# HGRN2 levels in 32-row blocks, S5 input products in three fp32r passes, a re-cut head and moved side steps in a hybrid decoder block on one core

## The chip, the cores and the metric

The kernel runs on one core of one Trainium2 chip. The metric is the device time of one execution in microseconds (us); smaller is better. TensorE (PE) multiplies, VectorE (DVE), ScalarE (ACT) and GpSimd (POOL) work on tensors, SyncE (SP) issues most DMAs.

## What is computed

One layer of a decoder on x of 256 tokens by 2048 features, in float32:

```
h = RMSNorm(x); [q|f|i|g | u | sq|sk|sv | 3 gates] = h @ w_in     # 8 groups of 512, gates 3 x 2048
o_a = hgrn2(q, f, i, g)          # gated linear recurrence, 4 heads of 128
o_b = s5(u): bu = Bbar u per group of 16 channels (64 complex states); x_t = Abar x_{t-1} + bu_t
             y = Re(C x) + D u; GLU(gelu(y))
o_c = stick_breaking(sq, sk, sv) # w = exp(log sigmoid(z) + suffix sums of log(1 - sigmoid(z))), strictly causal
x = x + (sum_k sigmoid(gate_k) * (o_k @ w_branch[k])) @ w_out
x = x + (silu(conv(up1)) * conv(up2)) @ w_down,  up = RMSNorm(x) @ w_up
```

## The kernel before

All large products are split in two parts, fp32r high and low: for each weight block PE multiplies high by high, high by low and low by high. Weights come in pieces of 128x1024 through a ring of four buffers. For piece p SP loads `raw` (it waits until the low part of piece p-4 is made), ACT copies it into `w_hi` (it waits until PE has used piece p-4), DVE subtracts into `w_lo`, and PE waits for `lo_ready` of p+1. An output tile of 128 columns of w_in takes two pieces, 2n and 2n+1.

The stages in order: a head (tiles 0 to 3 interleaved, as x and the first pieces land), tiles 4 to 7, tiles 8 to 79 (tiles 32 to 79 are the gates), GLU, branches, w_out, w_up with the convolution, w_down. In the first 80 tiles the whole of the three mixers is done beside the projection, by an order written out by hand. Each engine has a function `mixers(n)`:

- PE calls `mixers(n)` behind tile n. The table AT says behind which tile each small product stands: the HGRN2 levels lev0 to lev8 behind tiles 12, 14, ... 28, hg_o 30, the stick-breaking scores z0 and z1 37, the suffix sums within0 and within1 41, sb_o 44, the S5 input products bu0 and bu1 43, then bu2 to bu7 at 51, 59, 67, the S5 outputs s5_y0 to s5_y3 at 50, 58, 66, 74. Each of them writes one of two PSUM pairs and is taken from it by ACT or DVE.
- ACT and DVE call `mixers(n+1)` at the end of their step n. Step n of ACT is: high parts of pieces 2n+4 and 2n+5, the reading of tile n (Copy, or Sigmoid for gates), `mixers(n+1)`. Step n of DVE is: low parts of the same two pieces, for n under 16 the reading of tile n, `mixers(n+1)`. So what stands in ACT's `mixers(42)` is ahead of the high parts of pieces 88 and 89 (tile 44), and DVE's `mixers(43)` is behind the low parts of these two.
- Each engine executes its queue in order. `link` (and `run` on ACT, `tt`, `ts`, `stt` on DVE) also waits for the instruction just issued.

The sine and cosine tables of S5 (four groups g of 128x1024) are made at the tiles of TABLE_AT: three DVE steps, and then on ACT in `mixers` of the fourth number the sine group (Sin, Abs, Sin, with a table load ahead).

What the prediction follows, by line: `level(k)` and `fp32_product` on PE (L413), the S5 input products (L539), the warm-up products (L559), the high parts (L711), `run` (L721), the reading of tiles (L739), the exponentials of the levels (L779, L780), the z copies (L813), the low parts (L1024), `tt`, `ts` and `stt` (L1048, L1051, L1055), the level factors (L1227, L1228), the reading of levels into NEAR (L1243, L1245), the subtraction of `within` (L1314).

Of the kernel before, what the change touches and what calls it, by code (L numbers as in the profile page):

```python
# [45 lines left out]
P = 128  # L46
HALF = P // 2
D_MODEL = 2048
SEQ = 256
# [53 lines left out]
TABLE_AT = [(20, 21, 22, 23), (24, 25, 26, 27), (28, 29, 30, 31), (50, 51, 58, 59)]  # L103
# [5 lines left out]
HEAD_LOADS = [("x", 0), ("w", 0, 0), ("x", 1), ("w", 1, 0), ("x", 2), ("w", 2, 0), ("x", 3), ("w", 3, 0),  # L109
              ("w", 0, 1), ("w", 1, 1), ("x", 4), ("x", 5), ("w", 2, 1), ("w", 3, 1), ("x", 6), ("x", 7)]  # L110

HEAD_SPLITS = [("x", 0), ("w", 0, 0), ("x", 1), ("x", 2), ("x", 3), ("w", 1, 0), ("x", 4), ("x", 5), ("w", 2, 0), ("x", 6), ("x", 7),
               ("w", 3, 0), ("w", 0, 1), ("w", 1, 1), ("x", 8), ("x", 9), ("x", 10), ("x", 11), ("w", 2, 1), ("w", 3, 1), ("p", 4),
               ("x", 12), ("x", 13), ("x", 14), ("x", 15)]

HEAD_STEPS = [(5, 6, 7), (8,), (9,), (10, 11)]
WARM = 13
# [15 lines left out]
def layer(nc, xT, w_in, w_glu, w_br, w_out, w_up, w_down, norm_mix, norm_ffn, hg_gain, s5_small, s5_b, s5_c,  # L133
          s5_skip, sb_gain, conv, out):
    ctx = ExitStack()
    with ctx:
# [13 lines left out]
        level_mask = sb("level_mask", [P, LEVELS, HALF], U8)  # L150
        eye_half = sb("eye_half", [P, HALF])
# [9 lines left out]
        root = sb("root", [P, SEQ])  # L161

# [63 lines left out]

        def product(name):
            return pair[M[name] % 2]
# [53 lines left out]

        block = ctx.enter_context(nc.Block())
# [5 lines left out]
        def _(sp):  # L289
# [13 lines left out]
            def w_half(p, q):  # L303
                w = slice(q * HALF_PIECE, (q + 1) * HALF_PIECE)
                sp.dma_start(raw[p][:, w], w_in[head_source(p), :, w]).then_inc(raw_landed[p] if q else S(f"w_half{p}"), 16)

            for kind, *which in HEAD_LOADS:
                (x_part if kind == "x" else w_half)(*which)
# [37 lines left out]
        def _(pe):  # L346
# [75 lines left out]
            def level(k):  # L422

                if k == 0:
                    pe.wait_ge(S("hg_k"), 1)
                    group_ready(pe, HG_Q)
                    ops = [((j * HALF, (j + 1) * HALF, (4 * b + h) * HALF, (4 * b + h + 1) * HALF),
                            T4[2][:, h, (2 * b + j) * HALF:(2 * b + j + 1) * HALF],
                            group(HG_Q)[:, h, (2 * b + j) * HALF:(2 * b + j + 1) * HALF], True, True)
                           for b in range(2) for h in range(HEADS) for j in range(2)]  # L430
                else:
                    pe.wait_ge(S("hg_factors"), 2 * k)
                    W = T4[4 + k % 2]
                    if k < LEVELS - 1:
                        ops = [((j * HALF, (j + 1) * HALF, (4 * b + h) * HALF, (4 * b + h + 1) * HALF),
# [1293 lines left out]
```

## Time and profile before

| | |
|---|---|
| median of 3 runs | 1402.94 us (1402.54 to 1403.33) |
| profiled execution, its own time | 1402.92 us |
| span of that execution, first to last instruction | 1401.4 us |
| busy share of the span | PE 99%, PE weight loads 92%, DVE 74%, ACT 54%, POOL 10% |
| chain that ended last | PE 91%, DVE 6%, ACT 2%, DMA 1% |
| read from HBM | 258.66 MB, 186 GB/s over the span |

An engine's busy time is the union of its instructions; PE's matmuls overlap one another, so a busy PE is not one at its peak. The chain is followed back from the last instruction to what released it. "<-" in a row stands between what is written and what is read, and between an idle time and what ended it.

### The profile page before, as it was taken

How to read it: one execution, taken by the hardware profiler on the slowest of the kernel's cores; microseconds unless marked ns; L12 is line 12 of the kernel's file. 1: busy time of each engine (PE TensorE's matmuls, PEld its weight loads, DVE VectorE, ACT ScalarE, POOL GpSimd, SP SyncE). 2: the span in 40 equal slices, each digit the busy share in tenths (PEclk: the TensorE clock that was granted, in tenths of full speed). 3: DMA queues.
4: the chain of work that ended last, by engine and by line, in shares of the span. 5: the costliest groups of instructions: out<-in, count | busy, mean ns of one | idle time of the engine just before them, and what ended most of it. 6: DMA issues, size and time to landing. Idle time of an engine off the chain costs nothing.

```text
span 1401.4 us, 27481 instructions
## 1 busy us (share of the span) xinstructions
PE 1394.3 (99%) x9682; PEld 1285.5 (92%) x9682; DVE 1030.6 (74%) x1409; ACT 754.0 (54%) x1050; POOL 143.4 (10%) x190
## 2 busy tenths in 40 slices
PE   9999999999999999999999999999999999999999
PEld 8999999999999999988888888888888888888888
DVE  7898866699898777776687777777777776445453
ACT  7584777654543454545555555555555554344332
POOL 1200000000000014322111111111111110000000
PEclk9999999999999999999999999999999999999999
DMA  8654545454555556665556656656656656666663
GB/s 280 191 181 168 162 153 184 147 168 165 189 178 174 195 171 223 223 192 194 170 197 196 189 186 192 192 180 193 191 187 193 190 177 194 208 185 202 194 206 109
DMA packets 75935, 261.66 MB, mean 187 GB/s; under 512 B 8736, under 2 KB 9280, under 8 KB 75872
## 3 DMA queue, kind: packets, MB, share of 16 engines
q1 hardware_dynamic: 74304, 256.41, 57.0%
q0 software_dynamic: 1424, 4.37, 1.1%
q8 instruction: 44, 0.72, 0.2%
q14 instruction: 19, 0.16, 0.0%
q10 hardware_dynamic: 144, 0.01, 0.0%
HBM read 258.66 MB, written 2.10 MB: 186 GB/s over the span
## 4 chain that ended last, share of the span: by engine, by line
PE 91%; DVE 6%; ACT 2%; DMA 1%; issue 0%; SPq 0%; ACTq 0%; DVEq 0%
PE bank L354 40%; PE bank L368 22%; PE bank L356 21%; PE bank L394 5%; DVE w_lo L1024 2%; PE pair L413 1%; PE bank L379 1%; DVE a_in L1257 0%; ACT gates L721 0%; ACT w_hi L711 0%; DMA x_first<-xT 0%; DVE tmp L1055 0%; DVE tmp L1048 0%; DVE x_first L1217 0%; ACT tmp L721 0%
## 5 line engine op out<-in xcount | busy, mean ns | idle before, releaser
L1024 DVE TENSOR_TENSOR w_lo<-raw,w_hi 128x1024 fp32r<-128x1024 f32 x496 | 584.6, 1189 | 305.3 <-ACT w_hi L711 301.5
L711 ACT ACTIVATE w_hi<-raw 128x1024 fp32r<-128x1024 f32 x496 | 508.3, 1030 | 417.0 <-PE bank L356 198.9
L354 PE MATMUL bank<-h,w_hi 128*128 128x512 f32 x1408 | 488.4, 390 | 0.0
L356 PE MATMUL bank<-h,w_lo 128*128 128x256 f32 x1408 | 397.1, 282 | 0.0
L368 PE MATMUL bank<-a_in,w_hi 128*128 128x256 f32 x2048 | 363.1, 281 | 0.5 <-DVE w_lo L1024 0.5
L368 PEld LDWEIGHTS bank<-a_in,w_hi 128*128 128x128 f32 x2048 | 311.8, 188 | 5.3 <-issue 4.6
L354 PEld LDWEIGHTS bank<-h,w_hi 128*128 128x128 f32 x1408 | 264.2, 188 | 55.4
L368 PE MATMUL bank<-a_in,w_lo 128*128 128x256 f32 x1024 | 285.5, 279 | 0.0
L356 PEld LDWEIGHTS bank<-h,w_lo 128*128 128x128 f32 x1408 | 266.1, 189 | 0.0
L354 PE MATMUL bank<-act,w_hi 128*128 128x512 f32 x660 | 228.8, 390 | 0.0
L368 PEld LDWEIGHTS bank<-a_in,w_lo 128*128 128x128 f32 x1024 | 192.5, 188 | 0.0
L356 PE MATMUL bank<-act,w_lo 128*128 128x256 f32 x660 | 186.1, 282 | 0.0
L354 PEld LDWEIGHTS bank<-act,w_hi 128*128 128x128 f32 x660 | 123.8, 188 | 26.0
L356 PEld LDWEIGHTS bank<-act,w_lo 128*128 128x128 f32 x660 | 124.7, 189 | 0.0
L1653 POOL TENSOR_TENSOR padded<-sum_u,rstd 128x256 f32<-128x256 f32 x88 | 73.7, 838 | 413.3 <-DVE sum_u L1045 400.5
L354 PE MATMUL bank<-a_in,w_hi 128*128 128x512 f32 x256 | 88.8, 390 | 0.0
L356 PE MATMUL bank<-a_in,w_lo 128*128 128x256 f32 x256 | 72.2, 282 | 0.0
L964 ACT ACTIVATE silu<-convd 128x256 f32<-128x256 f32 x43 | 17.9, 417 | 96.0 <-DVE convd L1512 96.0
L1510 DVE SCALAR_TENSOR_TENSOR convd<-padded,taps,convd 128x256 f32<-128x256 f32 x88 | 62.6, 712 | 1.0 <-ACT convd L984 1.0
L1512 DVE SCALAR_TENSOR_TENSOR convd<-padded,taps,convd 128x256 f32<-128x256 f32 x88 | 53.9, 613 | 11.5
L354 PEld LDWEIGHTS bank<-a_in,w_hi 128*128 128x128 f32 x256 | 48.0, 188 | 10.0
L718 ACT ACTIVATE half<-bank 128x256 f32<-128x256 f32 x135 | 49.2, 365 | 3.8 <-PE bank L356 3.7
(222 smaller groups left out, 1370.3 us busy)
## 6 DMA issues: line engine op xcount, KB each, us to landing
raw<-w_up SPq DMA_DIRECT2D x176, 512.0 KB, 3.8
raw<-w_in SPq DMA_DIRECT2D x156, 512.0 KB, 4.3
raw<-w_down SPq DMA_DIRECT2D x80, 512.0 KB, 4.2
raw<-w_out SPq DMA_DIRECT2D x32, 512.0 KB, 4.2
raw<-w_br SPq DMA_DIRECT2D x16, 512.0 KB, 3.5
raw<-w_br SPq DMA_DIRECT2D x16, 256.0 KB, 3.4
raw<-w_down SPq DMA_DIRECT2D x16, 256.0 KB, 2.7
x_first<-xT SPq DMA_DIRECT2D x8, 256.0 KB, 6.6
```

The lines of the kernel that those rows point to most:

```text
L354: pe.matmul(bank[b][:, :], w[:, k * P:(k + 1) * P], a.rearrange("p a t -> p (a t)"), start=first and n == 0, stop=False, skip_group_check= ...
L356: mm = pe.matmul(bank[b][:, 0:SEQ], l[:, k * P:(k + 1) * P], a[:, 0, :], start=False, stop=last and n == len(blocks) - 1, skip_group_check ...
L368: mm = pe.matmul(bank[n % BANKS][:, 0:SEQ], x[:, k * P:(k + 1) * P], src[:, PIECE * h + k, part, :], start=h == 0 and k == 0 and m == 0, s ...
L379: mm = pe.matmul(bank[b][:, 0:SEQ], x[:, k * P:(k + 1) * P], rhs(k, part), start=first and k == 0 and m == 0, stop=last and k == blocks - ...
L394: mm = pe.matmul(bank[b][:, 0:SEQ], x[:, cols], src[:, k, part, :], start=k == 0 and m == 0, stop=k == CT - 1 and m == 2, skip_group_check ...
L711: act_e.activation(w_hi[s][:, 0:blocks * P], raw[s][:, 0:blocks * P], ACT.Copy).then_inc(hi_ready, 1)
L718: act_e.activation(half[j % 2][:, :], bank[j % BANKS][:, SEQ:2 * SEQ], ACT.Copy).then_inc(half_copied, 1)
L964: act_e.activation(silu[:, :], convd[:, (j - 3) % 4, :], ACT.Silu).then_inc(S("silu_done"), 1)
L1024: ve.tensor_tensor(w_lo[s][:, w], raw[s][:, w], w_hi[s][:, w].bitcast(F32), ALU.subtract).then_inc(lo_ready, 1)
L1510: ve.scalar_tensor_tensor(c, padded[:, j % 2, 1:SEQ + 1], taps[:, t, 1:2], c, ALU.mult, ALU.add).then_inc(S("tap1"), 1)
L1512: ve.scalar_tensor_tensor(c, padded[:, j % 2, 0:SEQ], taps[:, t, 0:1], c, ALU.mult, ALU.add).then_inc(S("conv_done"), 1)
L1653: pool.tensor_tensor(padded[:, j, 2:], sum_u[:, j, :], rstd[:, :], ALU.mult).then_inc(S("up_scaled"), 1)
```

## The change

- **Levels.** Levels 0 to 5 are computed in blocks of 32 rows and 32 columns (32 matmuls in four column groups where there were 16 of 64 in two). Level 6 has 16 products of 32x32 that are copied straight into the tile of scores, level 7 spreads over two column groups. Masks and NEAR are half as large, ACT's copies into the tile of scores go from two of 64 rows at tile 26 to four of 32 rows at tile 25, and POOL clears two more corners.
- **S5 input products.** s5_bT and u are split into high and low parts in the buffers of the soft-plus (two ACT copies, two DVE subtractions), and each product is three fp32r passes where it was one float32 one.
- **Suffix sums.** Two products of 128 columns with `ones` become one of 256 for each part.
- **Output splits.** The high and low parts of o_hg and o_sb, made at tiles 47 and 48, are made at tiles 75 and 77 (their buffers overlap those of the soft-plus).
- **Side steps.** sb_ln moves from `mixers(38)` on ACT behind the high parts of the next two pieces. The S5 angle moves from tile 12 to 15, sine and cosine of it from 13 to 16, the input gain from 15 to 17, the input weights from 17 and 19 to 19. The phase steps and sine groups of tables 1 and 2 move by TABLE_AT; table 3 lies in other buffers.
- **Head.** The first halves of four pieces are cut into quarters (`first_load`: 256 columns, semaphore first_landed), four of the eight issued from ACT's queue (HEAD_LOADS_2) before its first table load. PE does k blocks 0 and 1 of the four tiles, then 2 and 3, then 4 to 7. DVE makes the first high part of x by itself. Two fewer warm-up products.

```diff
-TABLE_AT = [(20, 21, 22, 23), (24, 25, 26, 27), (28, 29, 30, 31), (50, 51, 58, 59)]
+TABLE_AT = [(20, 21, 22, 23), (24, 25, 28, 29), (34, 37, 38, 42), (50, 51, 58, 59)]
...
+HEAD_LOADS = [("x", 0), ("f", 1, 0), ("f", 3, 0), ("x", 1), ("f", 1, 1), ("f", 3, 1), ("x", 2), ("w", 0, 1), ("x", 3), ("w", 1, 1),
+              ("x", 4), ("x", 5), ("w", 2, 1), ("w", 3, 1), ("x", 6), ("x", 7)]
+HEAD_LOADS_2 = [(0, 0), (2, 0), (0, 1), (2, 1)]
...
+HEAD_SPLITS = [("f", 0, 0), ("x", 1), ("f", 1, 0), ("f", 2, 0), ("f", 3, 0), ("x", 2), ("f", 0, 1), ("x", 3), ("f", 1, 1), ("f", 2, 1), ("f", 3, 1),
+               ("x", 4), ("x", 5), ("x", 6), ("x", 7), ("w", 0, 1), ("w", 1, 1), ("x", 8), ("x", 9), ("x", 10), ("x", 11), ("w", 2, 1), ("w", 3, 1),
+               ("p", 4), ("x", 12), ("x", 13), ("x", 14), ("x", 15)]
 
 HEAD_STEPS = [(5, 6, 7), (8,), (9,), (10, 11)]
-WARM = 13
+WARM = 11
...
+                def blocks(keys, queries):
+
+                    return [((i * QUARTER, (i + 1) * QUARTER, (4 * b + h) * QUARTER, (4 * b + h + 1) * QUARTER),
+                             keys[:, h, (4 * b + i) * QUARTER:(4 * b + i + 1) * QUARTER],
+                             queries[:, h, (4 * b + i) * QUARTER:(4 * b + i + 1) * QUARTER], True, True)
+                            for b in range(2) for h in range(HEADS) for i in range(4)]
...
-                    if k < LEVELS - 1:
-                        ops = [((j * HALF, (j + 1) * HALF, (4 * b + h) * HALF, (4 * b + h + 1) * HALF),
-                                W[:, h, (2 * b + j) * HALF:(2 * b + j + 1) * HALF],
-                                W[:, h, (2 * b + j) * HALF:(2 * b + j + 1) * HALF], True, True)
+                    if k < LEVELS - 2:
+                        ops = blocks(W, W)
+                    elif k < LEVELS - 1:
+                        ops = [((2 * j * QUARTER, (2 * j + 1) * QUARTER, (4 * b + h) * QUARTER, (4 * b + h + 1) * QUARTER),
+                                W[:, h, (4 * b + 2 * j) * QUARTER:(4 * b + 2 * j + 1) * QUARTER],
+                                W[:, h, (4 * b + 2 * j + 1) * QUARTER:(4 * b + 2 * j + 2) * QUARTER], True, True)
                                for b in range(2) for h in range(HEADS) for j in range(2)]
                     elif k < LEVELS:
-                        ops = [((0, HALF, (4 * b + h) * HALF, (4 * b + h + 1) * HALF), W[:, h, 2 * b * HALF:(2 * b + 1) * HALF],
-                                W[:, h, (2 * b + 1) * HALF:(2 * b + 2) * HALF], True, True) for b in range(2) for h in range(HEADS)]
+                        ops = [((b * HALF, (b + 1) * HALF, h * HALF, (h + 1) * HALF), W[:, h, 2 * b * HALF:(2 * b + 1) * HALF],
+                                W[:, h, (2 * b + 1) * HALF:(2 * b + 2) * HALF], True, True) for h in range(HEADS) for b in range(2)]
...
+                        second = out_[:, 0:512].rearrange("p (i t) -> p i t", i=2)[:, :, P:SEQ]
+                        for e, x in enumerate(parts):
+                            mm = pe.matmul(second, ones[:, :], x[:, 512:768].rearrange("p (i t) -> p i t", i=2), start=False, stop=e == 1,
+                                           skip_group_check=True)
...
-                            wait_taken(pe, "s5_bT")
-                            group_ready(pe, S5_U)
+                            pe.wait_ge(S("s5_split_lo"), 2)
...
+                        for m, (w, u) in enumerate(((0, 0), (0, 1), (1, 0))):
...
+                                    mm = pe.matmul(outs_[i // 2][:, at:at + SEQ], s5_w[w][rows, r, c, :], s5_u[u][rows, c, :],
+                                                   start=m == 0, stop=m == 2, skip_group_check=True)
...
+                    pe.wait_ge(S("w_first_lo"), BANKS * q + n + 1)
+                    piece(n, None, n, range(2 * q, 2 * q + 2), lambda k: a_raw_block(n, 2 * q + k), q == 0, False)
+            for n in range(BANKS):
+                piece(n, n, n, range(4, 8), lambda k: a_raw_block(n, 4 + k), False, False).then_inc(piece_used, 1)
...
+                if n == 16:
+                    act_e.wait_ge(S("s5_r"), 1)
+                    run("s5_sin", s5v("sin"), s5v("r"), ACT.Sin)
+                    run("s5_absr", s5v("t2"), s5v("r"), ACT.Abs)
+                    run("s5_cos", s5v("cos"), s5v("t2"), ACT.Sin, scale=-1.0, bias=half_pi[:, 0:1])
+                if n == AT["lev5"] + 3:
+                    wait_taken(act_e, "lev5")
+                    act_e.wait_ge(S("hg_levels"), LEVELS - 2)
+                    for i in range(4):
+                        rows = slice(i * QUARTER, (i + 1) * QUARTER)
+                        act_e.activation(T2[6][rows, :, rows], NEAR[rows, :, :], ACT.Copy).then_inc(S("hg_within"), 1)
...
-                    run("sb_ln", LOG1P, LOG1P, ACT.Ln, bias=1.0)
...
                     run("sb_wexp", Z, Z, ACT.Exp)
+                    group_ready(act_e, S5_U)
+                    run("s5_split_hi", softp_hi[:, 0:1024], flat(UU), ACT.Copy)
+                    wait_taken(act_e, "s5_bT")
+                    run("s5_split_hi", softp_lo[:, 0:1024], s5_bT[:, :, :, :].rearrange("p r c s -> p (r c s)"), ACT.Copy)
...
-                if n == AT["sb_o"] + 3:
+                if n == AT["s5_y3"] + 1:
+                    wait_product(act_e, "bu7")
+                    act_e.wait_ge(S("s5_x"), 4 * CT)
...
+                if n == AT["z0"] + 1:
+                    run("sb_ln", LOG1P, LOG1P, ACT.Ln, bias=1.0)
...
+                if n == 15:
                     s5_angle()
-                if n == 15:
+                if n == 17:
                     s5_input_gain()
-                if n == 17 or n == 19:
-                    s5_input_weights((n - 17) // 2)
+                if n == 19:
+                    for r in range(2):
+                        s5_input_weights(r)
...
-                            ins = ve.tensor_tensor(NEAR, ps, bc(eye_half[:, :].unsqueeze(1), full), ALU.mult)
+                            ins = ve.tensor_tensor(NEAR, ps, bc(eye_quarter[:, :].unsqueeze(1), full), ALU.mult)
+                        elif k < LEVELS - 2:
+                            ins = ve.copy_predicated(NEAR, bc(level_mask[:, k:k + 1, :], full), ps)
                         elif k < LEVELS - 1:
-                            ins = ve.copy_predicated(NEAR, bc(level_mask[:, k:k + 1, :], full), ps)
+                            issue(ve.tensor_copy(T2[6][0:QUARTER, :, QUARTER:HALF], ps[0:QUARTER, :, :]), "hg_far")
+                            ins = ve.tensor_copy(T2[6][HALF:HALF + QUARTER, :, HALF + QUARTER:P], ps[HALF:HALF + QUARTER, :, :])
                         elif k < LEVELS:
-                            ins = ve.tensor_copy(T2[6][0:HALF, :, HALF:P], ps[0:HALF, :, :])
...
+                    ve.wait_ge(S("s5_split_hi"), 2)
+                    tt("s5_split_lo", softp_hi[:, 1024:2048], flat(UU), softp_hi[:, 0:1024].bitcast(F32), ALU.subtract)
+                    tt("s5_split_lo", softp_lo[:, 1024:2048], s5_bT[:, :, :, :].rearrange("p r c s -> p (r c s)"),
+                       softp_lo[:, 0:1024].bitcast(F32), ALU.subtract)
                     ve.wait_ge(S("sb_wexp"), 1)
                     causal("sb_w", Z)
...
-                if n == AT["sb_o"] + 4:
+                if n == AT["s5_y3"] + 3:
```

## Rows read from the trace of the kernel before

**Rows 1.** The page's table of engines, first entry: busy us (share) xinstructions.

```profile
PE 1394.3 (99%) x9682; PEld 1285.5 (92%) x9682; DVE 1030.6 (74%) x1409; ACT 754.0 (54%) x1050; POOL 143.4 (10%) x190
```

**Rows 2.** The list of waits of PE: us in total, times, longest us.

```profile
PE pair L413 <- DVE tmp L1228: 1.6, 3, 1.2
...
PE bank L354 <- DVE w_lo L1403: 0.9, 1, 0.9
PE bank L368 <- DVE w_lo L1024: 0.5, 1, 0.5
```

**Rows 3.** Busy time by stretches: stretch, length, then PE, PEld, DVE, ACT, POOL (xinstructions), granted clock.

```profile
99.40:102.60 3.20, 3.20 (x30) 3.20 (x29) 2.72 (x16) 1.46 (x3) 0.00 (x0) 1.00 0.81 239
158.50:172.70 14.20, 14.08 (x142) 13.67 (x140) 13.87 (x19) 7.92 (x12) 0.00 (x0) 1.00 0.46 143
59.95:109.10 49.15, 47.97 (x452) 47.36 (x451) 47.70 (x86) 38.18 (x51) 0.00 (x0) 1.00 0.51 165
257.70:277.20 19.50, 18.98 (x161) 18.29 (x158) 18.99 (x23) 8.91 (x12) 0.00 (x0) 1.00 0.57 185
```

**Rows 4.** The chain of waits of the whole run: start us, us, what.

```profile
12.99 4.42 DMA raw<-w_in
...
121.66 1.08 PE pair L413 x32
122.74 11.41 PE bank L368 x96
134.15 0.87 PE pair L419 x8
...
510.07 67.20 PE bank L394 x576
```

**Rows 5.** The same chain from 243 to 300 us.

```profile
243.69 2.63 PE pair L413 x16
...
270.37 2.29 PE pair L413 x16
272.67 11.20 PE bank L368 x96
283.86 1.07 PE pair L539 x16
```

**Rows 6.** Timeline of ACT from 245 to 262 us: start, us, what [idle before].

```profile
250.05 1.49 ACT L721 ACTIVATE tmp<-tmp 128x1536 f32<-128x1536 f32 x1
...
252.85 1.49 ACT L721 ACTIVATE tmp<-tmp 128x1536 f32<-128x1536 f32 x1
254.37 2.01 ACT L711 ACTIVATE w_hi<-raw 128x1024 fp32r<-128x1024 f32 x2
```

**Rows 7.** Timeline of ACT from 262 to 289 us.

```profile
277.31 1.28 ACT L721 ACT_TABLE_LOAD   x1 [5.37 <-DVE tmp L1314]
278.60 1.49 ACT L721 ACTIVATE tmp<-tmp 128x1536 f32<-128x1536 f32 x1
```

**Rows 8.** Timeline of DVE from 254 to 287 us.

```profile
257.74 3.54 DVE L1055 SCALAR_TENSOR_TENSOR tmp<-tmp 128x1536 f32<-128x1536 f32 x2
...
275.42 1.81 DVE L1314 TENSOR_TENSOR tmp<-tmp,pair 128x768 f32<-128x768 f32 x2
281.21 2.36 DVE L1024 TENSOR_TENSOR w_lo<-raw,w_hi 128x1024 fp32r<-128x1024 f32 x2 [3.98 <-ACT w_hi L711]
283.49 1.80 DVE L1048 TENSOR_TENSOR tmp<-tmp,upper 128x256 f32<-128x256 f32 x4
```

**Rows 9.** Timeline of ACT from 202 to 212 us.

```profile
205.12 1.28 ACT L721 ACT_TABLE_LOAD   x1
206.41 2.15 ACT L721 ACTIVATE gates<-gates 128x1024 f32<-128x1024 f32 x2
208.59 1.15 ACT L721 ACTIVATE gates<-gates,half_pi 128x1024 f32<-128x1024 f32 x1
```

**Rows 10.** Timeline of PE from 0 to 7 us.

```profile
1.24 5.53 PE L559 MATMUL pair<-ones 128*128 128x128 f32 x26 [1.24 <-POOL ones L1585]
```

More of the change, by code:

```diff
@@ L426, in level @@
                     group_ready(pe, HG_Q)
-                    ops = [((j * HALF, (j + 1) * HALF, (4 * b + h) * HALF, (4 * b + h + 1) * HALF),
-                            T4[2][:, h, (2 * b + j) * HALF:(2 * b + j + 1) * HALF],
-                            group(HG_Q)[:, h, (2 * b + j) * HALF:(2 * b + j + 1) * HALF], True, True)
-                           for b in range(2) for h in range(HEADS) for j in range(2)]
+                    ops = blocks(T4[2], group(HG_Q))
                 else:
@@ L858, in _ @@
             act_e.dma_start(gain_mix[:, :], norm_mix).then_inc(S("gains_landed"), 16)
+            for which in HEAD_LOADS_2:
+                first_load(act_e, *which)
             act_e.wait_ge(S("ones"), 1)
@@ L878, in _ @@
                     a_raw_hi(*which)
+                elif kind == "f":
+                    w_first_hi(*which)
                 elif kind == "w":
@@ L1155, in masks @@
                 ve.wait_ge(S("iota"), 4)
-                diff, xor = T[4][:, 0:P].bitcast(I32), T[4][:, P:P + HALF].bitcast(I32)
-                place, row = T[4][:, 2 * P:2 * P + HALF].bitcast(I32), T[4][:, 3 * P:3 * P + HALF].bitcast(I32)
-                upper_half = T[4][:, 4 * P:4 * P + HALF]
+                diff, xor = T[4][:, 0:P].bitcast(I32), T[4][:, P:P + QUARTER].bitcast(I32)
+                row, part = T[4][:, 2 * P:2 * P + QUARTER].bitcast(I32), T[4][:, 3 * P:3 * P + QUARTER].bitcast(I32)
+                above = T[4][:, 4 * P:4 * P + QUARTER]
                 if step == 0:
@@ L1162, in masks @@
                 if step == 1:
-                    ts("masks", row, row, float(HALF), float(HALF), ALU.is_ge, ALU.mult)
-                    tt("masks", row, place, row, ALU.subtract)
-                    tt("masks", upper_half, xor, row, ALU.is_gt)
-                    tt("masks", eye_half[:, :], xor, row, ALU.is_equal)
+                    for size in (HALF, QUARTER):
+                        ts("masks", part, row, float(size), float(size), ALU.is_ge, ALU.mult)
+                        tt("masks", row, row, part, ALU.subtract)
+                    tt("masks", above, xor, row, ALU.is_gt)
+                    tt("masks", eye_quarter[:, :], xor, row, ALU.is_equal)
                     link(ve, ve.tensor_tensor(xor, xor, row, ALU.bitwise_xor), "masks")
```

121 lines of the change are left out of this document (67 added, 54 removed).

## The prediction

> **What bounds the kernel now.** The first view to read is the page's table of engines: TensorE (PE) has work in flight for 99% of the span [rows 1]. Time is therefore gained only where a matmul gets cheaper or where PE waits, and lost wherever a new wait appears. The second view is the list of waits: PE's own waits are few and short, 1.6 us behind VectorE (DVE) for the HGRN2 level factors, 0.9 us in the head, and 0.5 us for a low part of weights [rows 2]. The third view is the chain of work that ended last. It mostly runs through PE, but between 59 and 110 us, 147 and 186 us, and 246 and 264 us it leaves PE and goes through DVE and ScalarE (ACT). There PE is only just fed: in 59.95 to 109.10 DVE is busy for 47.70 of 49.15 us, in 158.5 to 172.7 for 13.87 of 14.20, and in 257.7 to 277.2 for 18.99 of 19.50 [rows 3]. What the change puts into, or takes out of, these stretches counts in full. The sum below is made against the profiled run's own 1402.92 us (span 1401.4 us plus 1.5 around it), which is the median of the three shown to 0.02 us.
>
> **The head (first 20 us).** The start is re-cut: quarter pieces of weights, half of them issued from ACT's queue, two fewer warm-up products, k blocks 0 and 1 of all four tiles first. This can remove the 0.9 us wait [rows 2]. But PE meets a later gate: the load at 12.99 us took 4.42 us to land, and its high and low parts come after it [rows 4]. That load is still issued only after the low part of the first piece, which in the new order comes at about the same time. Nearest is therefore no gain, the other end is the whole 0.9. I take -0.3 us, range 0 to -1.0.
>
> **HGRN2 levels on PE.** A level is 32 matmul records on 64 columns in two column groups and takes 1.08 us [rows 4]. Levels 0 to 5 become 64 records on 32 columns in four column groups. If the columns set the pace, about half of it (0.47 us) goes; if a record costs the same however short, nothing goes; if the number of instructions sets it, a level costs 0.9 us more. No row shows 32-column products, so I choose -0.3 us a level, nearest to the pace of the columns: for levels 0 to 4, 5 x 0.3 = -1.5 us (range -2.4 to +4.5). The Trainium skill (TensorEngine Tiling (Array Packing), Instruction Overhead) says that a matmul pays some 60 cycles however few its columns. By that rule levels 0 to 4 would gain nothing and the sum below would be 1.5 us higher; no row of before has so short a product.
>
> **Level 2's wait.** The DVE work before level 2 loses the input gain of S5, 3.2 us of small instructions from 99.4 to 102.6 us [rows 3], which moves from tile 15 to 17, behind the level's factors; the angle moves within the stretch and is neutral. The readings of levels 0 and 1 also get shorter. So the wait of 1.2 us [rows 2] goes: -1.2 us. What is late next there is nothing: PE itself gains less than these 3.2 us.
>
> **Levels 5 to 8.** From 158.5 to 172.7 us DVE runs without a gap up to the factors of level 7 [rows 3], and this stretch starts from PE's tile 22 and ACT's table of sines at tile 23, which stays. So what PE gains in levels 5 and 6 it waits for at level 7; only about 0.1 us of DVE work goes: -0.1 us. Level 7 itself goes from one column group to two: -0.4 us (0 to -0.5). The sine group of tile 27 moves to 29, behind level 8's factors, and with it the rest of the 1.6 us of waits: -0.2 us. Up to the z products at 243.69 us the sum is -0.3 - 1.5 - 1.2 - 0.1 - 0.4 - 0.2 = -3.7 us.
>
> **From the z products to the first S5 input product.** Here I choose to follow the instructions one by one, since everything is in the order of ACT's and DVE's queues. Before: z at 243.69, first S5 product at 283.86, which waited for nothing late [rows 5].
> - sb_ln moves behind the high parts of two pieces (2.01 us, [rows 6]). DVE then starts its softplus when ACT has done those two and the logarithm: 251.55, the end of the first exponential, + 2.05 for the two high parts + 1.28 for the table load [rows 7] + 1.50 for the logarithm [rows 6] = 256.4, where before it started at 257.74 [rows 8]: 1.35 us earlier. From there to the subtraction of `within` (275.42 + 1.81) DVE has no gap [rows 3, 8], so all of that, and ACT's exponential after it, comes 1.35 us earlier: the exponential ended at 280.1 [rows 7] and will end at 278.7. The 0.5 us wait near 264 us [rows 2] goes, and so do four of the sixteen matmuls of `within` (2.29 us [rows 5]; at 0.119 us each, from 96 in 11.41 us [rows 4], 0.45 us); both only make PE wait longer at what follows.
> - In the same place of ACT's queue (mixers(42)) come now two copies of 128x1024 for the S5 splits, as long as a high part, about 1.07 us each with the wait of `link`, and behind them the sine group that stood at tile 31: table load 1.28, then 2.15 and 1.15 with their gaps 3.36 us [rows 9]. Added: 2.15 + 4.65 = 6.8 us. Queued behind it are the high parts of pieces 88 and 89. They start at 278.7 + 6.8 = 285.5 instead of 280.12 [rows 7, 8].
> - DVE's mixers(43) stand behind the low parts of those two pieces; they began at 283.49 [rows 8] and will begin 5.4 us later, at 288.9. Only then come the two low splits, at half of 2.36 us each plus the link [rows 8], 2.5 us: 291.4. PE waits for both (s5_split_lo of 2) before the first S5 product, and its whole queue stands behind that wait.
> - PE's tiles 42 and 43 (11.20 us, [rows 5]) end at about 282.6 in these coordinates. So PE **waits 8.9 us** where it waited for nothing, and starts the product 7.7 us later than before.
> - The product: 16 records in 1.07 us [rows 5] become 24 single-pass ones, by the columns 0.2 us less (bounds: 0.4 more, if each costs what one did, to 0.3 less). To its end: +7.7 - 0.2 = +7.5 us. The three later ones: -0.6 us.
>
> **The clock.** PE's first 26 records on 128 columns took 5.53 us, 0.213 us each [rows 10]; eight later ones took 0.87 us, 0.109 each [rows 4]. The granted clock reads 1.00 in all windows, but by these durations PE ran at 1.2 GHz at first, after having done nothing, and at 2.4 GHz later. No row shows PE idle for 8.9 us inside the kernel; its longest wait was 1.2 us, and the tiles after it ran at 0.119 us a matmul [rows 2, 4]. Bounds: 0, or half of those 5.53 us. An idle time of 8.9 us is nearer to the start than to 1.2 us: +2.3 us. The Trainium skill (TensorE: Matmul & The Clock Gate, Part 1) also says that an idle array goes back to half rate.
>
> **At no cost.** The splits of the outputs (two copies and two subtractions, 4.4 us on two engines) move to tiles 75 to 77; their readers begin at 510 us [rows 4], some 20 us later. The fourth sine table waits for sb_o, long done. The other small DVE moves lie beside PE tiles with room; if that room were gone each would cost what it lasts, 1 to 3 us.
>
> **Sum.** -3.7 + 7.5 - 0.6 + 2.3 = +5.5 us, **1408.4 us**.
>
> **Rivals.**
> - *The clock stays up* over the wait: 1408.4 - 2.3 = 1406.1. For it: the windows show 1.00 everywhere. Chance 0.20; with some larger gains in head and levels it ends within 0.2%.
> - *Short products are not cheaper*: levels gain nothing, +1.5 to +2 us, 1410; were they bound by instructions, +6 us, 1414.4. Chance 0.15. This is what the rule cited above would do here.
> - *Faster: the wait at the first S5 product is not there*, or ACT and DVE have their work done in time. Then the gains stand, and with them the wait near 264, `within` and the product itself (0.5 + 0.4 + 0.2): -3.7 - 0.6 - 1.1 = -5.4 us, 1397.5. It decides the sign as soon as that wait is under 2.6 us instead of 8.9. For it: in the kernel before ACT stands idle for 5.37 us just ahead of the exponential [rows 7], room in which a sine group would fit. Against it: in the queue the group stands behind the exponential, and not ahead of it. Chance 0.10.
> - *The head and the level waits don't give what I say* (DVE's stretch starts no earlier): up to 1.5 us more, 1410. Chance 0.10.
>
> **How the numbers follow.** The forecast has 0.45. The range leaves out the faster rival and the dearest levels: its low end has the clock up, 0.7 us more from the head and 0.8 more from levels and 1.5 for an S5 chain shorter than I read it (1403.0), its high end the levels at no gain, half a microsecond more of clock and 1.5 for the head and waits (1412.0). About 0.2% (2.8 us) is what a measurement of this kernel tells from no change. Faster by more than that: 0.10, the one rival. Within: 0.18, from the clock that stays with larger gains. Slower: 0.72.
>
> **What would show it.** In the list of waits a new first row of PE behind DVE for the S5 product (L539's successor) of 8 to 9 us, at about 279 us on the new time axis; ACT busy from the exponential through two copies and the sine group without a high part between them; the matmuls after it at about twice their time for some 5 us. Level products of 64 records in 0.6 to 0.9 us; no wait at level 2 and level 8, one of some 0.7 us at level 7. The prediction is wrong if PE's wait at the S5 product is under 5 us, or if the levels take over 1.1 us.

## The result, and the profile after

| | before | after |
|---|---|---|
| median of the runs beside each other | 1402.94 us (9 runs, 1402.14 to 1403.45) | **1406.75 us** (9 runs, 1405.79 to 1407.55) |
| ratio | | 1.0027, 95% interval 1.0019 to 1.0036 |
| span of the profiled execution | 1401.4 us | 1405.3 us |
| mean granted clock in it | 1.000 | 0.996 |

The change makes the kernel 3.8 us (0.27%) slower. It was predicted as slower by 5.5 us, in a range of 1403.0 to 1412.0. PE's waits after the change, to be read against [rows 2] (engine and line, what it waited for: total us, times, longest):

```profile
PE pair L569 <- DVE softp_lo L1093: 8.8, 1, 8.8
PE pair L589 <- POOL ones L1657: 1.2, 1, 1.2
PE pair L432 <- DVE tmp L1276: 1.2, 3, 0.8
PE bank L373 <- DVE w_lo L1069: 0.3, 1, 0.3
```

One wait of 8.8 us has appeared, at the first S5 input product (L539 of before is L569 now). The waits for `w_lo` of 0.9 and 0.5 us are gone, one of 0.3 us is left, and the level factors still cost 1.2 us, though at other levels (0.2, 0.2 and 0.8 us at levels 3, 6 and 7).

ACT's queue in the stretch that was followed, after the change (start, duration, instruction, idle time before it and what ended that); it answers to [rows 7]:

```profile
270.96 1.28 ACT L750 ACT_TABLE_LOAD   x1 [4.91 <-DVE tmp L1369]
272.26 1.49 ACT L750 ACTIVATE tmp<-tmp 128x1536 f32<-128x1536 f32 x1
273.78 1.06 ACT L750 ACTIVATE softp_hi<-proj 128x1024 fp32r<-128x1024 f32 x1
274.87 1.06 ACT L750 ACTIVATE softp_lo<-s_bT 128x1024 fp32r<-128x1024 f32 x1
275.95 1.28 ACT L750 ACT_TABLE_LOAD   x1
277.25 2.15 ACT L750 ACTIVATE gates<-gates 128x1024 f32<-128x1024 f32 x2
279.43 1.15 ACT L750 ACTIVATE gates<-gates,half_pi 128x1024 f32<-128x1024 f32 x1
280.61 2.00 ACT L740 ACTIVATE w_hi<-raw 128x1024 fp32r<-128x1024 f32 x2
```

The exponential is at 272.26, then two S5 copies, then the sine group, and only then the high parts of pieces 88 and 89. DVE's answer to [rows 8], and PE's, from the chain that ended last (start, us, what):

```profile
281.70 2.36 DVE w_lo L1069 x2
284.06 1.15 DVE softp_hi L1093
285.23 1.24 DVE softp_lo L1093
286.51 1.65 PE pair L569 x20
288.16 7.95 PE bank L387 x48
296.11 2.62 PE pair L432 x16
298.73 33.61 PE bank L387 x288
...
340.05 39.40 PE bank L387 x336
```

[Rows 5] has the first S5 product at 283.86 in 1.07 us, with no wait. Here it starts at 286.51, takes 1.65 us, and tile 44 behind it takes 7.95 us. The reason for the last two stands in the granted clock. Stretches of the changed kernel (us, busy us and instructions of each engine, PE's granted clock, DMA share, GB/s):

```profile
277.60:282.00 4.40, 0.09 (x1) 0.00 (x0) 0.30 (x1) 4.30 (x5) 0.00 (x0) 1.00 0.00 0
282.00:286.00 4.00, 0.00 (x0) 0.00 (x0) 3.97 (x4) 3.97 (x5) 0.00 (x0) 0.58 0.41 129
286.00:289.50 3.50, 2.99 (x30) 2.77 (x31) 3.33 (x7) 0.47 (x2) 0.00 (x0) 0.50 0.42 157
289.50:293.00 3.50, 3.50 (x19) 3.50 (x18) 3.50 (x6) 0.00 (x0) 0.00 (x0) 0.52 0.65 179
293.00:297.00 4.00, 4.00 (x33) 3.92 (x32) 2.59 (x4) 1.85 (x2) 0.00 (x0) 1.00 0.29 113
```

A mean of 0.58 over 4 us is 3.4 us at half and the rest at full, so PE was granted 1.2 GHz from about 282.6 us on, 5 us after the end of its last matmul at 277.7 us, and by the 0.52 of the fourth row until about 292.9, over 6 us after it had begun to work again.

### The profile page after: what moved, and what is told of

It reads as the page before. It is cut to its first block, busy times and chain, and to the rows that moved or that the text cites. A ratio compares the mean times of both kernels' runs of the same rounds, so it can differ in the third digit from the quotient of the medians.

```text
span 1405.3 us, 27940 instructions
## 1 busy us (share of the span) xinstructions
PE 1391.0 (99%) x9898; PEld 1283.6 (91%) x9898; DVE 1033.7 (74%) x1419; ACT 755.0 (54%) x1055; POOL 144.4 (10%) x192
## 4 chain that ended last, share of the span: by engine, by line
PE 79%; DVE 1%; ACT 1%; issue 0%; ACTq 0%
PE bank L373 38%; PE bank L375 20%; PE bank L387 15%; PE bank L413 5%; PE bank L398 1%; DVE w_lo L1069 1%; PE pair L432 1%; PE pair L569 0%; ACT gates L750 0%; DVE softp_lo L1093 0%; DVE proj L1100 0%; DVE tmp L1369 0%; ACT tmp L750 0%; ACT L750 0%; DVE proj L1341 0%
## 5 line engine op out<-in xcount | busy, mean ns | idle before, releaser
L1033 ACT ACTIVATE act<-convd 128x256 f32 (+1 forms) x44 | 18.5, 420 | 62.2 <-DVE convd L1589 62.2
```

Source lines behind the costliest of these rows:

```text
L1033: act_e.activation(act[:, q, 0, :], convd[:, (j - 2) % 4, :], ACT.Copy).then_inc(S("act_hi"), 1)
```

## The experiments

Each kernel ran on a chip beside the kernel before, which had medians of 1402.91 to 1403.01 us in these sets.

| kernel | median, us | ratio to before, 95% |
|---|---|---|
| e1_sine55 | 1402.09 | 0.9986 to 1.0004 |
| e2_splits_early | 1400.09 | 0.9971 to 0.9989 |
| e3_both | 1395.95 | 0.9935 to 0.9962 |
| e4_no_s5 | 1401.77 | 0.9983 to 1.0001 |
| e5_busy | 1404.65 | 1.0003 to 1.0021 |
| e6_old_head | 1395.46 | 0.9933 to 0.9961 |
| e7_old_gain | 1397.23 | 0.9944 to 0.9971 |
| e8_tables | 1394.69 | 0.9929 to 0.9956 |
| e9_fp32_s5 | 1397.48 | 0.9945 to 0.9973 |
| e10_best | 1394.50 | 0.9925 to 0.9952 |
| e11_ln_old | 1396.96 | 0.9944 to 0.9971 |
| e12_after_again | 1407.13 | 1.0019 to 1.0041 |

### What the wait of 8.8 us is made of

**e1_sine55**: the sine group alone goes out of the way.

```diff
-TABLE_AT = [..., (34, 37, 38, 42), ...]
+TABLE_AT = [..., (34, 37, 38, 55), ...]
```

> The changed kernel with one move: its third group of sine tables goes from step 42 of ACT's queue to step 55. The result is complete. Theory (PE's wait of 8.8 us is the length of what was put into ACT's queue ahead of the high parts of pieces 88 and 89, namely the two S5 copies and the sine group): the high parts come 4.6 us earlier, so the wait at the first S5 input product falls from 8.8 to 4.2 us and the kernel takes 4.6 us less, 1402.1; if the granted clock no longer falls after the shorter wait, another 2.9 us less, 1399.2. Rival A (the wait comes from the S5 copies and subtractions alone, and the sine group stands in a gap of ACT): wait still 8 to 9 us, 1406.7. Rival B (sine group moved means the tables come too late for the states): a new wait at the states and about 1406.

Measured: 1402.09 us, and in its list of waits

```profile
PE pair L569 <- DVE softp_lo L1093: 4.2, 1, 4.2
```

The wait shrank by the 4.6 us of the sine group to the tenth, and the median by 4.7 us. Both rivals fall. The granted clock still fell, in the profiled execution for 3.4 us (0.57 over 282 to 286 us, 1.00 behind it); the product took 1.38 us and tile 44 6.95. So 1.3 us of the clock's cost went too, and the two spans differ by 5.4 us (1405.3 and 1399.9). In seven of the eleven executions the mean granted clock was lower (0.997 or 0.998) than in the profiled one (0.999), so in these the clock was low for longer. That the medians differ by just the length of the sine group is therefore in part luck.

**e2_splits_early**: the S5 parts are made ahead of the exponential, in ACT's idle 4.9 us.

```diff
 # ACT, mixers(42), shortened
+group_ready(act_e, S5_U); wait_taken(act_e, "s5_bT")
+for hh in range(2): wait_product(act_e, f"within{hh}")
+run("s5_split_hi", ...); run("s5_split_hi", ...)
 for hh in range(2): wait_taken(act_e, f"within{hh}")
 run("sb_wexp", Z, Z, ACT.Exp)
-group_ready(...); run("s5_split_hi", ...); wait_taken(...); run("s5_split_hi", ...)
 # DVE: the two s5_split_lo from mixers(43) to mixers(42), behind the subtraction of within
```

> The changed kernel with the sine group left at step 42, but ACT's two S5 copies ahead of the exponential of the SB weights, in the time in which ACT stood idle, and DVE's two subtractions for the low parts right behind the subtraction of the within products, before the low parts of pieces 88 and 89. The result is complete. Theory (queue order): the wait of 8.8 us at the first S5 input product is gone, PE waits about 2.3 us at the low part of piece 88 instead, which the sine group holds up, the clock stays at full rate; 1397.4. Rival A (ACT's idle time there is no room, since the copies delay the exponential and all behind it): about 2 us more, 1399.5. Rival B (any wait of 2 us brings the lower clock): 1400 or more.

**e4_no_s5**: the S5 products are float32 again, with no parts to be made; the sine group stays.

```diff
-pe.wait_ge(S("s5_split_lo"), 2)
+wait_taken(pe, "s5_bT"); group_ready(pe, S5_U)
-for m, (w, u) in enumerate(((0, 0), (0, 1), (1, 0))):      # three passes
+pe.matmul(outs_[i // 2][...], s5_bT[rows, r, c, :], group(S5_U)[rows, c, :], start=True, stop=True)   # one
...
-run("s5_split_hi", ...); run("s5_split_hi", ...)           # ACT
-tt("s5_split_lo", ...); tt("s5_split_lo", ...)             # DVE
```

> The changed kernel with the S5 input products as they were before: float32, 16 records each, no copies and no subtractions for them, and no wait for low parts. The sine group stays at step 42. The result is complete. Theory: the high parts of pieces 88 and 89 still stand behind the sine group (4.65 us) but not behind the two copies, and DVE has no 2.5 us of splits; the wait at the S5 product goes, one of about 2.1 us at the low part of piece 88 comes, the S5 products take 1.07 us instead of 0.91, the clock stays up: 1397.8. Rival (the sine group alone is the cause of the wait of 8.8 us): a wait of 6 us or more remains and the time is over 1402. Rival (the single-pass products themselves save much): over 1399 with no wait left.

Measured: 1400.09 and 1401.77 us, 2.7 and 4.0 us more than I expected. The wait at the S5 product is gone in both, as the theory says, and the wait for the low part of piece 88 is there with the length expected; what I had missed stands behind it. From the lists of waits, e2_splits_early and then e4_no_s5:

```profile
PE bank L387 <- DVE w_lo L1071: 2.4, 1, 2.4
```

```profile
PE bank L387 <- DVE w_lo L1065: 2.1, 1, 2.1
PE pair L432 <- DVE proj L1382: 1.8, 1, 1.8
```

The second wait of e4_no_s5 is sb_o's, behind tile 44: it needs the PSUM pair of the first S5 product. Its chain shows who held that pair:

```profile
278.98 1.06 ACT w_hi L740
...
280.07 2.36 DVE w_lo L1065 x2
...
285.32 1.22 DVE w_lo L1065
286.54 0.60 DVE proj L1379
...
288.34 0.61 DVE proj L1382
...
289.08 2.86 PE pair L432 x16
```

DVE reads the S5 product (L1379 to L1382) behind the low parts of four pieces, and the first of these waited for ACT's high parts behind the sine group. e3_both, without the sine group there, starts sb_o at 284.86 us. So a delay in ACT's queue of 4.6 us costs PE 4.2 us there, whether at one place or at two. In e2_splits_early PE reaches sb_o at nearly the same moment (289.12 us) without the 1.8 us, because the clock had fallen after the wait of 2.4 us (0.59 over 282 to 286 us) and tile 44 took longer. There the low clock cost nothing, since DVE held sb_o in either case: seven of the eleven executions of e2_splits_early have a mean clock of 0.999 and took 1399.38 to 1400.40 us, the four with 1.000 took 1399.79 to 1401.14. So its rival B comes near in number and is right about the clock in most executions, but the clock is not what the 2.7 us are. In the trace of e4_no_s5, with a wait of 2.1 us, the clock stayed at 1.00; six of its eleven executions have 0.999.

**e3_both**: both edits (the line of TABLE_AT as in e1_sine55, the moves as in e2_splits_early).

> Both edits at once: sine group at step 55, ACT's copies and DVE's subtractions for the S5 parts ahead of the high and low parts of pieces 88 and 89. The result is complete. Theory: nothing is left that PE waits for between the z products and the S5 input products; the sum of the changed kernel's gains alone remains, 1406.75 - 8.8 - 2.9 = 1395. Rival (the stretch is bound by DVE, so that what the splits add stays wherever they stand): 2.5 us more, 1397.5.

Measured: 1395.95 us, 0.95 over the 1395 expected. From the end of z to the end of sb_o it takes 45.75 us where the changed kernel takes 57.45; these 11.7 us are the 8.8 and 2.9 of the expectation. What is missing in the total lies elsewhere: 0.4 us ahead of z, where this trace is later (z ends at 241.72 against 241.28 us), and the rest between the profiled executions (11.2 us apart) and the medians (10.8). No wait is left between z and the S5 products. Its chain has the first S5 product behind tiles 42 and 43, and the tile behind it at its usual length:

```profile
278.14 0.91 PE pair L569 x22
279.05 5.81 PE bank L387 x48
284.86 2.62 PE pair L432 x16
```

DVE did not bound the stretch: the 2.5 us of low parts went into time in which it had waited. From e1_sine55 and e2_splits_early to e3_both it is 6.1 and 4.1 us. Between the changed kernel and this one lie 10.8 us, which is what a wrong place in two queues cost.

### What the clock costs

**e5_busy**: the wait stays, but PE works through it.

```diff
+outs_ = [start_product(f"bu{2 * c + e}") for e in range(2)]
 if c == 0:
+    for _ in range(39):
+        pe.matmul(outs_[0][:, 0:P], ones[:, :].bitcast(F32), ones[:, :].bitcast(F32), start=True, stop=True)
     pe.wait_ge(S("s5_split_lo"), 2)
```

> The changed kernel with the wait of 8.8 us left where it is, but TensorE kept at work during it: 39 float32 products of 128 columns of the ones (0.22 us each, 8.5 us in all) go into the output buffer of the first S5 input product ahead of the wait, and are overwritten. The result is complete. Theory (2.9 us of the loss are the clock alone, which falls because TensorE had done nothing): the granted clock stays at 1.00, tile 44 takes 5.7 instead of 7.86 us and the S5 product 0.9 instead of 1.65, 1406.75 - 2.9 = 1403.9. Rival (the lower clock has another cause, or the slow records after the wait are the pipeline's start): tile 44 still takes 7.8 us and the time stays 1406.7.

Measured: 1404.65 us, 2.1 us less than the changed kernel. The chain and a stretch of it:

```profile
287.96 5.81 PE bank L387 x48
293.77 2.79 PE pair L432 x16
```

```profile
286.00:289.50 3.50, 3.40 (x45) 3.08 (x45) 3.33 (x6) 0.94 (x2) 0.00 (x0) 1.00 0.49 186
```

The granted clock is 1.00 and tile 44 takes 5.81 instead of 7.95 us. Over whole executions the mean is 1.000 in all eleven of this kernel and 0.996 in all sixteen of the changed one. The rival falls: the loss behind the wait is the clock. Of the 2.14 us in tile 44 and 0.67 in the product, 0.17 came back in sb_o (2.79 for 2.62 us). That leaves 2.65 us between the two traces from the product's start on, and the medians show 2.1, 0.8 us less than expected. The missing half microsecond stands ahead of the product, which starts at 286.98 us here and at 286.51 in the changed kernel; where it comes from is the subject of the next run.

**e12_after_again**: the changed kernel once more.

> The changed kernel as it is, once more, beside the others: is its time the same where the first loads land otherwise? Theory (its profiled run had its first tiles 0.4 to 0.8 us earlier than the other runs with the same head): median 1406.75 to 1407.3, with its tile 6 starting at 19.0 to 19.4 us instead of 18.65, and the wait of 8.8 us as before. Rival (the early start belongs to the kernel): 1406.75, tile 6 at 18.65.

Measured: 1407.13 us (1406.41 to 1408.13). Where PE stands at the norm's product, behind tile 7, is a mark for the head. It can be held against the moment at which ACT starts on the first whole piece of the head (the load that the prediction has at 12.99 us), for whose landing it has waited. The changed kernel and then e12_after_again, PE's row and ACT's:

```profile
52.04 0.59 PE L432 MATMUL pair<-proj,ones 128*128 128x256 f32 x2
16.27 1.06 ACT L740 ACTIVATE w_hi<-raw 128x1024 fp32r<-128x1024 f32 x1 [1.42 <-DMA raw<-w_in]
```

```profile
52.71 0.59 PE L432 MATMUL pair<-proj,ones 128*128 128x256 f32 x2
16.94 1.06 ACT L740 ACTIVATE w_hi<-raw 128x1024 fp32r<-128x1024 f32 x1 [1.33 <-DMA raw<-w_in]
```

The same rows of five other traces:

| trace | head | ACT starts on the piece | PE's mark | between them |
|---|---|---|---|---|
| before | old | 17.44 | 53.20 | 35.76 |
| e6_old_head | old | 16.92 | 52.69 | 35.77 |
| e10_best | old | 17.01 | 52.77 | 35.76 |
| e3_both | new | 16.86 | 52.62 | 35.76 |
| e7_old_gain | new | 17.06 | 52.83 | 35.77 |

In all seven the mark follows that landing by 35.76 or 35.77 us, with the old head and with the new. So this load is the gate of the head, as the prediction suspected, and the early start of the first trace was its landing and no property of the kernel: theory holds, rival falls.

The same kernel is 0.67 us later at this mark in another execution, behind a wait of 1.1 us for the low part of a head piece that the first one did not have. Yet both spans are 1405.3 us. The chain of the second shows where that went:

```profile
287.23 1.65 PE pair L569 x20
288.88 7.22 PE bank L387 x48
```

```profile
289.50:293.00 3.50, 3.50 (x22) 3.50 (x22) 3.50 (x5) 0.00 (x0) 0.00 (x0) 0.65 0.46 110
```

PE's wait ended 0.72 us later, but the low clock was about 0.9 us earlier (0.65 over the last stretch is 2.45 us at half, to about 291.9 us, against 292.9), so less work fell into it and tile 44 took 7.22 instead of 7.95 us. The cost of the low clock is therefore no constant: here 2.2 us and in the first trace 2.9. The medians of the two sets less that of e5_busy give 2.1 and 2.5, with the 0.17 us at sb_o already taken off.

### The other steps of the sum

**e6_old_head**: e3_both with the head of before (loads, order of pieces, 13 warm-up products). PE's part of the edit, shortened:

```diff
-pe.wait_ge(S("w_first_lo"), BANKS * q + n + 1)
-piece(n, None, n, range(2 * q, 2 * q + 2), ...)
+if q == 0: pe.wait_ge(S("w_half_lo"), n + 1)
+mm = piece(n, n if q else None, n, range(4 * q, 4 * q + 4), ...)
```

> The version with both moves (third sine group at step 55, S5 parts early; 1395.95 us) with the head as it was before the change: half pieces from SyncE's queue alone, four blocks of one tile first, 13 warm-up products. The result is complete. Theory (the new head gives what the ends of tiles 4 to 12 show, 1.17 us, and all of it arrives at the end): 1397.1. Rival (stretches bound by VectorE between 59 and 172 us swallow it, as waits at levels 3, 6 and 7 that shrink by the same amount): 1396.0 to 1396.3.

Measured: 1395.46 us, 0.5 less than with the new head. Neither theory nor rival holds: nothing was swallowed further on, because there was nothing to swallow. At the mark above the old head stands at 52.69, (e10_best) 52.77 and (before) 53.20; the new one stands between 52.04 and 52.83 in its eleven traces, with 52.63 in the middle. The 1.16 us between the first two traces were one late and one early landing (17.44 and 16.27 us in the rows above).

**e7_old_gain**: e3_both with DVE's S5 setup at its old steps, and with it ACT's sine and cosine of the angle.

```diff
-if n == 15: s5_angle()
-if n == 17: s5_input_gain()
-if n == 19: for r in range(2): s5_input_weights(r)
+if n == 12: s5_angle()
+if n == 15: s5_input_gain()
+if n == 17 or n == 19: s5_input_weights((n - 17) // 2)
...
-if n == 16: run("s5_sin", ...)    # ACT
+if n == 13: run("s5_sin", ...)
```

> The version with both moves (1395.95 us) with VectorE's S5 setup where it was before the change: the angle at step 12, the input gain at 15, the input weights at 17 and 19. The result is complete. Theory (the input gain, 3.2 us of small instructions, ahead of level 2's factors was what level 2 waited for): the wait of 1.2 us or more at level 2 is back, 1397.2 to 1397.5. Rival (level 2 is ready in time because the shorter readings of levels 0 and 1 free VectorE): no wait at level 2, 1396.0. Rival (wait back, but swallowed by the wait at level 7): wait at level 2 and 1396.0.

Measured: 1397.23 us (1396.1 to 1398.04), 1.3 us more. Its waits at the levels:

```profile
PE pair L432 <- DVE tmp L1277: 2.9, 3, 1.4
```

In e3_both they come to 1.1 us in two. The wait of 1.4 us is level 2's, as expected, and there is a new one of 0.7 us at level 1, ahead of which the angle stands again. Both rivals fall. The step held, and the gain is 1.3 us by the medians and up to 2.3 (from the mark to z) by the profiled run, which was the slowest of the five. The moves were taken back together, so the run does not part the input gain from the angle and from ACT's sine group; for the input gain speaks the row of before, where its 3.2 us stand in DVE's queue ahead of level 2's factors [rows 3].

**e8_tables**: e3_both with the first two sine groups behind the levels.

```diff
-TABLE_AT = [(20, 21, 22, 23), (24, 25, 28, 29), (34, 37, 38, 55), (50, 51, 58, 59)]
+TABLE_AT = [(20, 21, 22, 29), (24, 25, 28, 47), (34, 37, 38, 55), (50, 51, 58, 59)]
```

> The version with both moves, and the first two sine groups later too: from step 23 to 29 and from 29 to 47, so that none stands in ScalarE's queue ahead of the factors of levels 6 and 7. The result is complete. Theory (the waits of 0.2 and 0.9 us at levels 6 and 7 are VectorE's and ScalarE's run that starts at the sine group of step 23): both go, 1395.95 - 1.1 = 1394.9. Rival (VectorE alone bounds that stretch, its 13.9 of 14.2 us being busy): the waits stay, 1395.9.

Measured: 1394.69 us, 1.3 less, and the rival falls. The only wait at a level that is left, level 3's:

```profile
PE pair L432 <- DVE tmp L1278: 0.2, 1, 0.2
```

**e9_fp32_s5**: e3_both with float32 S5 products (the edit of e4_no_s5).

> The version with both moves (1395.95 us) with the S5 input products as before the change: float32, 16 records each, no copies and no subtractions for them. The result is complete. It asks what the three-pass products are worth where nothing waits for their parts. Theory (their own time, plus what the run with float32 products showed: the tiles of 48 matmuls after such a product took 5.65 instead of 5.60 us until the next small product): four times 0.16 = 0.6 us and some 20 tiles at 0.05 = 1.0 us, 1397.6. Rival (the slower tiles came from the wait in that run, not from the products): 1396.6. Rival (the splits cost VectorE and ScalarE time that is missing elsewhere): 1395.9 or less.

Measured: 1397.48 us, 1.5 more, where the theory said 1.6. From its chain, to be held against the 39.40 us of the same 336 matmuls shown above (39.40 in e3_both too):

```profile
328.24 1.08 PE pair L569 x16
329.31 39.77 PE bank L387 x336
```

The seven tiles behind a float32 S5 product take 0.37 us longer than behind one of single passes. That holds for three groups (1.1 us); the four products themselves add 0.17 us each. The row of six tiles behind sb_o is as fast as before (33.61 us).

**e11_ln_old**: e3_both with the logarithm back in front of the high parts.

```diff
 run("sb_exp", LOG1P, LOG1P, ACT.Exp, scale=-1.0)
+run("sb_ln", LOG1P, LOG1P, ACT.Ln, bias=1.0)
...
-if n == AT["z0"] + 1:
-    run("sb_ln", LOG1P, LOG1P, ACT.Ln, bias=1.0)
```

> The version with both moves (1395.95 us) with the logarithm of the SB stretch back where it was before the change, ahead of the high parts of two pieces. The result is complete. Theory (VectorE's run from the softplus on starts 1.3 us later, and the wait of 0.5 us near 264 us comes back; nothing else on the path waits for it, since the S5 product now has over 3 us of room): 1396.4. Rival (the room hides it): 1395.95. Rival (the late run reaches the product of step 44 too): 1397.3.

Measured: 1396.96 us, 1.0 more. The wait for piece 82's low part is back:

```profile
PE bank L387 <- DVE w_lo L1070: 0.6, 1, 0.6
```

More is spread out: tiles 42 and 43 took 11.30 us together instead of 11.20, and sb_o took 2.86 instead of 2.62 us. So the late run does reach step 44, but for 0.2 to 0.3 us, and the result lies between the theory and the last rival.

**e10_best**: e8_tables with the head of before.

> The version with all sine groups later (1394.69 us) with the head as it was before the change. The result is complete. Theory (the new head is worth nothing that can be measured; the difference of 1.17 us between the two traces was where the first loads happened to land): 1394.2 to 1394.7. Rival (the head gives 1.17 us once the waits of levels 6 and 7 are gone, which swallowed it in the other version): 1395.9.

Measured: 1394.50 us against 1394.69, no difference that can be told; the theory holds. Both are 0.6% faster than the kernel before (0.9925 to 0.9952), with the same computation as the changed kernel.

## Why the prediction was right, point by point

- **The S5 chain** (the first product 7.7 us later against z, wait 8.9). z ends at 246.32 us in [rows 5] and at 241.28 in the trace after; the product starts at 283.86 and 286.51. That is 5.04 + 2.65 = 7.69 us. The wait is 8.82. By the prediction's own figures these would have been 7.5 (291.4 less 283.86) and 8.5 (tiles 42 and 43 ending at 283.86 less 0.5 and 0.45, so at 282.9 and not 282.6), so the agreement to a tenth is luck; that the chain is right to 0.3 us is not. The steps in between came as followed: DVE's softplus stands 10.10 us behind z instead of 11.42 (1.32 earlier, predicted 1.35), the high parts start at 280.61, the low ones at 281.70, then the two splits. e1_sine55 and e3_both take the wait apart into the two parts of the sum, 4.6 us for the sine group and 4.2 for the S5 parts.
- **The clock** (+2.3, chance 0.20 that it stays up). It fell; e5_busy shows that idleness was the reason. The size was 2.9 us in the first trace (0.74 in the product, 2.15 in tile 44), 2.2 in the second. That 2.3 lies so near is in part luck: its upper bound was half of the 5.53 us of the warm-up products, and the first trace is just over it, since PE worked for 6.4 us at the low clock there and for 4.7 us in the second.
- **The levels** (-0.3 us each). The step held, a little undersized: by the timelines, before and after, a level takes 1.15 us with 32 records of 64 columns and 0.76 with 64 records of 32, so PE gains 0.39 (the 1.08 of [rows 4] is the chain's, which leaves out the overlap with the tile). The bound in which a record costs the same however short is refuted: each column group has 16 records before and after, and one took 72 ns of the level with 64 columns and 48 ns with 32, neither the same nor half. By the Trainium skill (TensorEngine Tiling (Array Packing), Instruction Overhead), with some 60 cycles for a matmul however few its columns, the two would have been nearly alike if the cycles are counted by columns, as in the prediction; for these float32 products the trace disagrees. No run has the old levels in the new order, so the gain is read from these rows alone.

```profile
121.59 1.15 PE L413 MATMUL pair<-tmp 128*64 128x64 f32 x32
118.27 0.76 PE L432 MATMUL pair<-tmp 128*32 128x32 f32 x64 [0.21 <-DVE tmp L1276]
```

- **Level 2's wait** (-1.2). Right in place and about right in size (e7_old_gain: 1.4 us back there). The second row above shows what I had not named: a wait of 0.2 us at level 3.
- **Levels 5 to 8** (-0.1, -0.4 and -0.2, so -0.7). From the start of level 5 to z it is 95.99 us before (147.54 to 243.53) and 95.07 after (143.43 to 238.50), so -0.9. At level 7 there are 0.8 us of wait where I said 0.7, and level 8 waits for nothing.
- **The head** (-0.3). The first pair of traces shows -1.16 us, as if the step had been sized at a quarter of its worth. e6_old_head and e12_after_again show that it is worth nothing: between -0.1 us by the marks and +0.5 by the medians. The term was still too large, not too small. The prediction's own reading was the better one: the later gate is the load of the first whole piece, and "nearest is no gain" was right, the 0.3 taken all the same was not.
- **Behind tile 44** (-0.6). Three products gave 0.48, and 0.7 us more came from rows of seven tiles in a faster rhythm (39.40 instead of 39.77 us, twice). I had no term for this. The last 0.2 us are not the change's: the row of six tiles takes 33.61 instead of 33.84 us, but in the trace of before its tiles follow one another by 5.60 us as well, and the rest is one pause of 0.2 us near 321.4 us.
- **The output splits** at no cost: PE waits for nothing there in any of the traces.
- **The faster rival**. It said that the S5 wait would be absent and put 1397.5 us. What it describes is e3_both, in which the wait is absent because the order is another: 1395.95. The room of 5.4 us before the exponential was real, and only the order of the queue kept the change from using it.

By spans: -5.0 us up to z, +7.7 to the product, +0.6 in it, +2.1 in tile 44, -1.5 behind it, in all +3.9. The forecast of 5.5 was 1.6 us too high: 1.3 up to z and 0.9 behind tile 44, less 0.6 of clock. Of the 1.3 us up to z, 0.9 are the head (1.16 where 0.3 was forecast, and all 1.16 of it landing) and 0.5 the levels (3.87 us from the mark to z, where the terms come to 3.4). So the 3.9 us between these two traces hold 1.2 us of luck with the loads. The second execution of the changed kernel has 0.5 of it, and there a low clock that cost 0.7 us less made up for the rest (e12_after_again).

## What to carry to other kernels

Follow a moved step through the queue it is put into, with every instruction that then stands behind it, up to the next point at which that engine had room; here 6.8 us in ACT's queue and 2.5 in DVE's became 8.8 us of PE's, while 4.9 us of idle time lay just one instruction ahead. A wait that is taken away alone can come back at the next consumer of the same queue, so list all of them before you price it. Take differences of under a microsecond at the start of a kernel from several executions, never from one pair of traces.

## What the runs showed of the hardware that I had not expected

- The low clock does not end when PE works again. After the wait of 8.8 us it lasted 10.2 us in both traces of the changed kernel. In the first it was granted from about 282.6 us, 4.9 us after PE's last matmul, to about 292.9, with PE at work from 286.51. In the second it came 3.3 us after the last matmul, and its place against PE's work moved its cost from 2.9 to 2.2 us.
- It can also come when PE is already back at work. In e1_sine55 PE waited for 4.2 us and worked from 282.12 us on; the clock reads 1.00 over 282.12 to 282.45 us and 0.50 over 282.50 to 285.85. In e2_splits_early PE waited for 2.4 us and worked from 281.47 us on; the clock reads 1.00 over 281.47 to 282.70 us and 0.50 over 282.75 to 286.10. Each time it was low for 3.4 us.
- Whether a short wait brings it differs between executions of one kernel. The mean clock over an execution is 0.999 in seven of eleven of e2_splits_early (wait of 2.4 us) and in six of eleven of e4_no_s5 (waits of 2.1 and 1.8 us), and 1.000 in the others. In e3_both and the six kernels made from it, whose longest waits are 1.2 to 1.4 us, all executions have 1.000.
- A long row of equal matmuls ran in one of two rhythms, 39.40 or 39.77 us for 336, and kept it to the row's end. From one tile of 48 to the next that is 5.60 or 5.65 us. The rows behind a single-pass S5 product took 39.40 or 39.41 us, all 33 of them in eleven traces; those behind a float32 one took 39.77 in all three groups of e9_fp32_s5, in all three of e4_no_s5 and in two of three in the trace of before, where the first took 39.40. But the product's form does not settle it alone: behind sb_o, which is float32 in every kernel, the row of six tiles has the slow rhythm in one trace (e1_sine55, 33.92 us) and the fast one in the thirteen others. Why stays open.
- Where the load that gates the head lands differs by up to 0.8 us between executions of one head (16.27 to 17.06 us in the traces above), more than twice the 0.3 us at which the re-cut of the head was sized.
